# Latent attention in a decoder trunk: q left unnormalised until the exponential, the shared rotary key turned once, v copied by ScalarE, q and k signalled apart

## The chip, the core and the metric

The kernel runs on one core of a Trainium2 chip, in fp32. The metric is the device time of one execution in microseconds. A core has a matrix engine (TensorE, PE in the rows; its weight loads are listed apart as PEld), VectorE (DVE), ScalarE (ACT), GpSimd (POOL) and DMA queues, issued from SyncE (SP) and others. The engines run their own instruction streams and meet at semaphores: an instruction raises one, another engine waits until it has reached a count.

## The reference, cut to what matters

512 tokens of width 1024 pass through two layers. Layer 0 is a state-space and recurrent mixer, layer 1 is multi-head latent attention with 8 heads, and a mixture of 64 experts follows each. The change is inside the attention of layer 1:

```python
c_q = rms_norm(proj[..., :Q_LORA], cq_norm)                  # 384 wide
c_kv = rms_norm(proj[..., Q_LORA:Q_LORA + KV_LORA], ckv_norm)  # 256 wide
k_rope = proj[..., Q_LORA + KV_LORA:]                        # 64 wide, one for all heads
q = (c_q @ w_uq).reshape(bsz, seq, MLA_HEADS, QK_DIM)        # 8 heads of 128 + 64
kv = (c_kv @ w_ukv).reshape(bsz, seq, MLA_HEADS, NOPE_DIM + V_DIM)
k_nope, v = kv[..., :NOPE_DIM], kv[..., NOPE_DIM:]
k = jnp.concatenate([k_nope, jnp.broadcast_to(k_rope[:, :, None, :], ...)], axis=-1)
q = rms_norm(q, q_norm)      # one root for each token and head, over all 192
k = rms_norm(k, k_norm)
q = concat([q[..., :NOPE_DIM], apply_rope(q[..., NOPE_DIM:], cos, sin)])
k = concat([k[..., :NOPE_DIM], apply_rope(k[..., NOPE_DIM:], cos, sin)])
s = einsum(q, k) / sqrt(192); causal mask; p = softmax(s); o = p @ v
```

`apply_rope` turns the two halves of the last 64 columns: `[t1*c - t2*s, t1*s + t2*c]`.

## The kernel before

The 512 tokens are four chunks `c` of 128, one token per partition. Layer 0 and its experts run first, then `norm_tensor(2)` and `odd_tensor`, `odd_scalar`, `odd_vector`, which are the attention on TensorE, ScalarE and VectorE, then the experts of layer 1, whose weights stream from HBM.

The attention has four stages. First the input projection (line 872), with the low-rank parts normalised and transposed chunk by chunk (lines 961 to 977 and 1041 to 1047). Then, second, comes what the change is about, a list called `UNITS`. A unit is one PSUM bank of TensorE's work, and the banks are used in turn, eight of them, so that unit `u` waits until unit `u - 8` has been copied out (`copied`, line 861). For each chunk there are three units `q` (line 890, the 1536 columns of q), four units `kv` (line 894, each with k and v of two heads), and six units `t` (line 907), which transpose a finished chunk. TensorE runs q and kv of chunk `c` before `t` of chunk `c - 1`:

```python
        for c in range(TC + 1):
            if c < TC:
                UNITS += [("q", c, n) for n in range(3)] + [("kv", c, n) for n in range(4)]
            if c:
                UNITS += [("t", c - 1, n) for n in range(6)]
```

ScalarE copies the q units out (line 987), squares all of q (line 992), squares k once VectorE has copied it (line 995), squares the shared rotary key (line 997), takes the root for q and k together (line 1000), and copies the `t` units of the chunk before into the transposed q and k (lines 1005, 1007 and 1009). VectorE sums the squares of q (line 1053), copies k and v of the four kv units (lines 1059 and 1060), sums the squares of k (line 1063), and then, after the root, multiplies q and k by their roots, multiplies the rotary parts by the norm's weights and turns them, 12 tensor operations in all (lines 1072 to 1087). At the end of these, one semaphore, `s_qn`, tells that the chunk is done. TensorE waits for it ahead of `t` (line 898), and ScalarE waits for it ahead of the square of the next q (line 991), since the scratch `rt` of the rotation lies in the tile `sq` that the square writes.

The third stage is the 32 pairs of head and chunk, `n`. TensorE computes the scores (lines 923 to 925), VectorE takes the maximum and scales it (lines 1094 and 1097), ScalarE takes the exponential (line 1016) with that as its bias, VectorE divides by the sum (line 1104), TensorE transposes (line 933), ScalarE copies (line 1024), and TensorE multiplies with v (line 943). Before its first score TensorE waits until all `t` units are copied (line 909). The fourth stage is the output projection (line 441).

Three DMA issues hang on this: the weights of the output projection wait for the last kv unit (line 1815), the gains of the next norm wait for `s_qn` of the last chunk (line 1869), and the experts' first weights wait for the last score (line 1819).

Of the kernel before, what the change touches and what calls it, by code (L numbers as in the profile page):

```python
# [8 lines left out]
ALU = mybir.AluOpType  # L9
# [3 lines left out]
P = 128  # L13
# [9 lines left out]
H = 8  # L23
# [49 lines left out]
def hybrid_decoder(nc, a, out):  # L73
    ctx = ExitStack()
    with ctx:
# [657 lines left out]
        def even_gpsimd():  # L733
# [49 lines left out]
            for m in range(MT):  # L783
# [29 lines left out]
        rt = [sq[:, i * 512:(i + 1) * 512].rearrange("p (h d) -> p h d", h=2 * H) for i in range(3)]  # L813
# [5 lines left out]
                                      .rearrange("p (c d) -> p c d", c=TC) for i in range(4)]  # L819
        css, croot, crs = small(2), small(2), small(2)  # L820
# [17 lines left out]
        s_qn = sem("s_qn")  # L838
# [22 lines left out]
        def copied(u):  # L861

            kv = UNITS[u][0] == "kv"
            return (s_qv if kv else s_qa), sum((x[0] == "kv") == kv for x in UNITS[:u + 1])

        def odd_tensor():
# [11 lines left out]
            for u, (kind, c, n) in enumerate(UNITS):  # L878
# [17 lines left out]
                else:  # L896
                    if n == 0:
                        TE.wait_ge(s_qn, c + 1)
                    for j in range(4):
                        if n < 2:  # L900
                            src = qi[c % 2][:, 4 * n + j, 0:NOPE]
                        elif n < 4:
                            src = ki[c % 2][:, 4 * (n - 2) + j, :]
                        else:
                            src = rp[c % 2][:, 8 * (n - 4) + 2 * j:8 * (n - 4) + 2 * j + 2, :]\
                                .rearrange("p h d -> p (h d)")
                        last = TE.transpose(bank[:, j * P:(j + 1) * P], src, ident)
# [49 lines left out]
        def odd_scalar():  # L957
# [20 lines left out]
            for kind, c, n in UNITS:  # L978
                if kind == "kv":
                    continue  # L980
                u = unit(kind, c, n)
                bank = ps[:, u % 8, :]
                S.wait_ge(s_q, u + 1)
                if kind == "q":
# [3 lines left out]
                    if n == 2:  # L988
                        S.wait_ge(*copied(u))
                        if c:  # L990
                            S.wait_ge(s_qn, c)
                        S.activation(sq, qif[c % 2], ACT.Square).then_inc(s_hsq, 1)
                        S.wait_ge(s_hs, 3 * c + 1)
                        S.wait_ge(*copied(unit("kv", c, 3)))
# [4 lines left out]
                        S.wait_ge(s_hs, 3 * c + 3)  # L999
                        S.activation(hroot, hss, ACT.Sqrt, bias=eps, scale=1.0 / QK).then_inc(s_hr, 1)  # L1000
# [5 lines left out]
                elif n < 4:  # L1006
                    S.activation(kTn[:, 4 * (n - 2):4 * (n - 2) + 4, cc], src, ACT.Copy, scale=gnk).then_inc(s_qa, 1)
                else:
                    S.activation((qTr, kTr)[n - 4][:, :, cc], src, ACT.Copy).then_inc(s_qa, 1)
            for n in range(H * TC + 2):  # L1010
                if n < H * TC:
# [4 lines left out]
                    S.activation(pr[n % 3][:, 0:nk], ps[:, n % 3, 0:nk], ACT.Exp, scale=ATT_SCALE,  # L1016
# [9 lines left out]
        def odd_vector():  # L1026
# [13 lines left out]
            ts(ropec, ropec, -2.0, ALU.mult, 1.0, ALU.add)  # L1040
            for c in range(TC):
# [5 lines left out]
                V.nop().then_inc(s_cn, 1)  # L1047
            for c in range(TC):
# [3 lines left out]
                V.wait_ge(s_hsq, 3 * c + 1)  # L1052
                vlink(V.reduce_sum(hss[:, 0:8], sq.rearrange("p (h d) -> p h d", h=H), AX.X))
                V.nop().then_inc(s_hs, 1)
                for n in range(4):
                    u = unit("kv", c, n)
                    V.wait_ge(s_q, u + 1)
# [12 lines left out]
                rq = hrs[:, 0:8][:, :, None]  # L1070
# [4 lines left out]
                V.tensor_tensor(q_[:, :, 0:NOPE], q_[:, :, 0:NOPE], rq.to_broadcast([P, H, NOPE]), ALU.mult)  # L1075
                tt(k_, k_, rk.to_broadcast([P, H, NOPE]), ALU.mult)
                V.tensor_tensor(p_[:, 0:8, :], p_[:, 0:8, :], grq[:, None, :].to_broadcast([P, H, ROPE]), ALU.mult)
                tt(p_[:, 8:16, :], p_[:, 8:16, :], grk[:, None, :].to_broadcast([P, H, ROPE]), ALU.mult)
                cb = ropec[:, c:c + 1, :].to_broadcast([P, 2 * H, half])
                snb = ropes[:, c:c + 1, :].to_broadcast([P, 2 * H, half])  # L1080
                f1, f2 = p_[:, :, 0:half], p_[:, :, half:ROPE]
                V.tensor_tensor(rt[0], f1, snb, ALU.mult)
                tt(rt[1], f2, snb, ALU.mult)
                V.tensor_tensor(f1, f1, cb, ALU.mult)
                tt(f2, f2, cb, ALU.mult)
                V.tensor_tensor(f1, f1, rt[1], ALU.subtract)
                tt(f2, f2, rt[0], ALU.add)
                V.nop().then_inc(s_qn, 1)  # L1088
            for n in range(H * TC + 5):
                if n < H * TC:  # L1090
# [6 lines left out]
                    V.tensor_scalar(nb[:, b:b + 1], mx[:, b:b + 1], -ATT_SCALE, None, ALU.mult).then_inc(s_mx, 1)  # L1097
# [882 lines left out]
```

## Time and profile before

| | |
|---|---|
| time, 3 runs | 1644.01 us median, 1641.84 to 1645.41 |
| the profiled execution's own time | 1644.24 us |
| its span | 1642.3 us |
| TensorE busy in the span | 1351.0 us, 82% |
| units of stage two, first q to last copy | 849.94 to 943.9 us of the span |
| the 32 heads and chunks | 944.08 to 1025 us |
| output projection | from 1025.28 us |
| experts of layer 1, first expert | from about 1112 us to the end |

All starts are microseconds from the start of the span. An engine's busy share says little of the whole; what a change is worth is read from the stage in which it lies, by who waits for whom there. Idle time in square brackets stands for the time that the engine waited just before the row, with the row of another engine that released it.

### The profile page before, as it was taken

What the parts mean: (1) busy time and instruction counts of PE and PEld (TensorE: products, weight loads), DVE (VectorE), ACT (ScalarE), POOL (GpSimd) and SP (SyncE); (2) the same over time, 40 slices, a digit from 0 to 9 for tenths busy, and PEclk for the clock granted to TensorE, in tenths of its full rate; (3) what the DMA queues carried; (4) which work ended last, traced back from release to release, by engine and by line L of the source; (5) the groups of instructions that cost most, each with busy time, mean ns of one, the idle gap of its engine ahead of it and who ended that gap; (6) DMA issues with size and microseconds to landing.
All of it is one profiled execution on the core that took longest, in us unless ns stands there. A gap on an engine that the chain in (4) does not pass through costs nothing.

```text
span 1642.3 us, 19412 instructions
## 1 busy us (share of the span) xinstructions
PE 1351.0 (82%) x6152; PEld 632.2 (38%) x6152; DVE 490.5 (30%) x940; ACT 287.3 (17%) x564; POOL 316.6 (19%) x427
## 2 busy tenths in 40 slices
PE   5988995988777878788889699977988787878786
PEld 4555453333223333333544376453333232333332
DVE  6996125111111111112507654142111111111114
ACT  3235110111001010101243443111111000010100
POOL 6213001232221212121000000002332222212220
PEclk9999996999999998989889799988999999999988
DMA  6514724999999999997220301366999999999995
GB/s 210 211 46 151 298 97 160 394 387 406 402 402 399 405 395 413 401 399 290 99 109 1 116 1 63 142 256 247 393 401 401 392 402 394 409 404 403 389 382 235
DMA packets 83522, 472.36 MB, mean 288 GB/s; under 512 B 13970, under 2 KB 16194, under 8 KB 32912
## 3 DMA queue, kind: packets, MB, share of 16 engines
q1 hardware_dynamic: 69792, 445.25, 68.7%
q0 software_dynamic: 11952, 20.14, 3.8%
q10 hardware_dynamic: 1728, 6.29, 0.9%
q8 instruction: 33, 0.54, 0.1%
q14 instruction: 17, 0.14, 0.0%
HBM read 454.59 MB, written 27.39 MB: 293 GB/s over the span
## 4 chain that ended last, share of the span: by engine, by line
PE 43%; SPq 31%; DVE 13%; issue 6%; DMA 5%; ACT 2%; DVEq 0%; POOL 0%; ACTq 0%; POOLq 0%
SPq L1600 20%; PE ps L1395 14%; SPq L1605 11%; PE ps L1415 6%; DMA ring<-in_moe_w 4%; PE ps L441 3%; PE ps L1385 2%; PE ps L872 2%; PE ps L315 2%; PE ps L390 2%; PE ps L430 2%; DVE ring L541 1%; PE ps L925 1%; PE ps L943 1%; DVE extra L541 1%
## 5 line engine op out<-in xcount | busy, mean ns | idle before, releaser
L1395 PE MATMUL ps<-ring,region_b 128*64 128x512 f32 x1408 | 342.3, 642 | 79.7 <-issue 53.7
L1395 PEld LDWEIGHTS ps<-ring,region_b 128*64 128x64 f32 x1408 | 116.3, 148 | 303.1 <-issue 265.7
L1532 DVE TENSOR_TENSOR extra<-extra,ps 128x256 f32<-128x256 f32 x64 | 27.0, 421 | 609.5 <-ACT extra L1470 609.5
L1395 PE MATMUL ps<-wbuf,region_b 128*64 128x512 f32 x320 | 165.6, 678 | 48.3 <-DMA region_a<-in_moe_w 29.1
L1415 PE MATMUL ps<-ring,extra 128*64 128x512 f32 x704 | 160.8, 598 | 34.2 <-DVE extra L1538 34.2
L1395 PE MATMUL ps<-region_a,region_b 128*64 128x512 f32 x320 | 165.8, 678 | 0.0
L1339 POOL DMA_INDIRECT region_b<-hrow,icol x120 | 111.2, 927 | 148.2 <-issue 148.2
L1351 POOL DMA_INDIRECT ytok<-extra,icol x120 | 105.6, 880 | 154.1 <-issue 154.1
L1470 ACT ACTIVATE extra<-ps 128x256 f32<-128x256 f32 x64 | 24.6, 384 | 593.0 <-PE ps L1395 593.0
L1545 DVE COPY extra<-ps 128x512 f32<-128x512 f32 x64 | 44.3, 692 | 242.2 <-PE ps L1415 242.2
L1395 PEld LDWEIGHTS ps<-wbuf,region_b 128*64 128x64 f32 x320 | 48.2, 156 | 160.6 <-issue 150.1
L1415 PEld LDWEIGHTS ps<-ring,extra 128*64 128x64 f32 x704 | 49.8, 136 | 114.8 <-issue 89.7
L1349 POOL COPY icol<-blkidx 64x2 int32 x60 | 10.5, 175 | 421.4 <-DVE extra L1545 421.4
L1385 PEld LDWEIGHTS ps<-con,region_b 128*128 128x128 f32 x512 | 63.2, 195 | 64.3 <-issue 64.3
L1385 PE MATMUL ps<-con,region_b 128*128 128x128 f32 x512 | 75.7, 292 | 13.6 <-DMA region_b<-hrow,blkidx 13.6
L1415 PE MATMUL ps<-wbuf,extra 128*64 128x512 f32 x320 | 73.1, 597 | 16.7 <-DVE extra L1538 16.7
L1476 ACT ACTIVATE extra<-ps 128x512 f32<-128x512 f32 x64 | 38.2, 597 | 276.1 <-PE ps L1415 276.1
L315 PE MATMUL ps<-region_b,wbuf 128*128 128x512 f32 x128 | 55.8, 594 | 0.0
L1463 ACT ACTIVATE region_b<-ps 128x512 f32<-128x512 f32 x64 | 38.2, 597 | 81.5 <-PE ps L1385 81.5
L1839 POOL DMA_DIRECT2D gain<-in_p_norms x4 | 2.4, 600 | 252.1 <-DVEq L1088 168.7
L1527 DVE COPY region_b<-ps 128x512 f32<-128x512 f32 x64 | 44.3, 692 | 18.5 <-PE ps L1385 18.3
L1395 PEld LDWEIGHTS ps<-region_a,region_b 128*64 128x64 f32 x320 | 48.1, 156 | 0.0
(297 smaller groups left out, 1568.6 us busy)
## 6 DMA issues: line engine op xcount, KB each, us to landing
ring<-in_moe_w SPq DMA_DIRECT2D x264, 1024.0 KB, 26.3
wbuf<-in_moe_w SPq DMA_DIRECT2D x80, 1024.0 KB
region_a<-in_moe_w SPq DMA_DIRECT2D x40, 1024.0 KB
ytok<-ring SPq DMA_DIRECT2D x8, 1024.0 KB, 10.2
wbuf<-in_ev_w_in SPq DMA_DIRECT2D x3, 2048.0 KB, 17.2
wbuf<-in_ev_w_out SPq DMA_DIRECT2D x2, 2048.0 KB, 14.2
hrow<-region_a ACTq DMA_DIRECT2D x8, 512.0 KB, 10.8
region_a<-ytok SPq DMA_DIRECT2D x8, 512.0 KB, 5.3
```

The costliest lines, as they stand in the source:

```text
L315: last = TE.matmul(ps[:, bank, :], w[:, k, m * P:(m + 1) * P], hT[:, k, :], start=k == 0, stop=k == KC - 1)
L441: last = TE.matmul(ps[:, 4 + (n + 2) % 4, :], lhs(k, n // 2), wout[n % 2][:, k, :], start=k == 0, stop=k == KC - 1)
L1339: G.indirect_dma_start(xin[j][CAP * g:CAP * g + n, :], None, hrow[l], bass.IndirectOffsetOnAxis(ap=icol[0:n, 2 * j + g:2 * j + g + 1], axi ...
L1351: G.indirect_dma_start(ytok[l], bass.IndirectOffsetOnAxis(ap=icol[0:n, 4 + 2 * j + g:5 + 2 * j + g], axis=0), yo[j][CAP * g:CAP * g + n, : ...
L1385: last = TE.transpose(ps[:, k // 4, (k % 4) * PAIR:(k % 4 + 1) * PAIR], xin_block(j, k), ident)
L1395: last = TE.matmul(ps[CAP * g:CAP * (g + 1), 2 + j, :], xtr[j][:, k, CAP * g:CAP * (g + 1)], up_weights(2 * slot + g, k), start=k == 0, st ...
L1415: last = TE.matmul(ps[CAP * g:CAP * (g + 1), 6 + nh, :], hidT[j][:, f, CAP * g:CAP * (g + 1)], w2[2 * slot + g][:, f * D + nh * 512:f * D ...
L1463: S.activation(xtr[j][:, 4:8, :].rearrange("p k s -> p (k s)"), ps[:, 1, :], ACT.Copy)\
L1527: V.tensor_copy(xtr[j][:, 0:4, :].rearrange("p k s -> p (k s)"), ps[:, 0, :])\
L1545: V.tensor_copy(yo[j][:, 0:512], ps[:, 6, :]).then_inc(ml["s_ye"][l], 1)
L1600: nc.sync.dma_start(w13[b][:, n, :], src).then_inc(s, 16)
L1605: nc.sync.dma_start(w2[b], src).then_inc(s, 16)
```

## The change

It has five parts.

- q is no longer multiplied by its root. The scores come out of TensorE too large by it, and since a query is a partition there, the root goes in as the exponential's scale, one number per partition, `scl[:, n:n + 1]` in place of a constant, and as the factor of the maximum (`nscl`). Two operations of 128x8 for each chunk fill these tables.
- The norm's weights on the rotary part of q go into four tables (`qcc`, `qss`, `qcs`, `qsc`), made once. The rotation of q is then 6 operations of 128x256 that read the q copied out and wait for no root. Its scratch `rt` lies in `cbuf`, no longer in `sq`.
- The shared rotary key is weighted and turned once for all four chunks and before any root (`krot`, 8 operations of 128x128). For each chunk one operation of 128x512 spreads it over the heads with their roots.
- v is copied out by ScalarE, after VectorE has copied k of the same bank. All units then count on one semaphore, `s_qa`.
- `s_qn` is raised when q is turned, ahead of the sums for k, and a new one, `s_kn`, when k is scaled. The `t` units are reordered to q, q, rotary q, k, k, rotary k, and TensorE waits for `s_qn` ahead of the first and for `s_kn` ahead of the fourth. ScalarE's square of the next q waits for `s_hs`, the counter of VectorE's sums, and no longer for `s_qn`. The root (`keys_root`) moves behind the first two `t` copies of the chunk before, except for chunk 0.

The diff, cut to its core:

```diff
-        rt = [sq[:, i * 512:(i + 1) * 512].rearrange("p (h d) -> p h d", h=2 * H) for i in range(3)]
+        rt = [cbuf[:, i * 256:(i + 1) * 256].rearrange("p (h d) -> p h d", h=H) for i in range(2)]
+        scl, nscl = extra[:, 4032:4064], extra[:, 4064:4096]
...
         def copied(u):
 
-            kv = UNITS[u][0] == "kv"
-            return (s_qv if kv else s_qa), sum((x[0] == "kv") == kv for x in UNITS[:u + 1])
+            return s_qa, u + 1
...
-                    if n == 0:
-                        TE.wait_ge(s_qn, c + 1)
+                    if n % 3 == 0:
+                        TE.wait_ge((s_qn, s_kn)[n // 3], c + 1)
...
+            def keys_root(c):
+                S.wait_ge(s_hs, 3 * c + 3)
+                S.activation(hroot, hss, ACT.Sqrt, bias=eps, scale=1.0 / QK).then_inc(s_hr, 1)
...
                         if c:
-                            S.wait_ge(s_qn, c)
+                            S.wait_ge(s_hs, 3 * c)
                         S.activation(sq, qif[c % 2], ACT.Square).then_inc(s_hsq, 1)
+                    continue
+                if kind == "kv":
+                    kvs += 1
+                    S.wait_ge(s_qv, kvs)
+                    S.activation(vbuf[:, c, 2 * n * VD:(2 * n + 2) * VD].rearrange("p (h d) -> p h d", h=2),
+                                 bank.rearrange("p (h d) -> p h d", h=2)[:, :, NOPE:NOPE + VD], ACT.Copy)\
+                        .then_inc(s_qa, 1)
+                    if n == 3:
                         S.wait_ge(s_hs, 3 * c + 1)
-                        S.wait_ge(*copied(unit("kv", c, 3)))
                         S.activation(sq[:, 0:H * NOPE], kif[c % 2], ACT.Square).then_inc(s_hsq, 1)
...
-                        S.wait_ge(s_hs, 3 * c + 3)
-                        S.activation(hroot, hss, ACT.Sqrt, bias=eps, scale=1.0 / QK).then_inc(s_hr, 1)
+                        if c == 0:
+                            keys_root(c)
...
+                if n == 1 and c + 1 < TC:
+                    keys_root(c + 1)
...
-                    S.activation(pr[n % 3][:, 0:nk], ps[:, n % 3, 0:nk], ACT.Exp, scale=ATT_SCALE,
+                    S.activation(pr[n % 3][:, 0:nk], ps[:, n % 3, 0:nk], ACT.Exp, scale=scl[:, n:n + 1],
...
+            V.wait_ge(s_ct, TC)
+            V.tensor_tensor(k1, kro[:, :, 0:half], gains(grk, 0), ALU.mult)
+            tt(k2, kro[:, :, half:ROPE], gains(grk, 1), ALU.mult)
...
-                    V.tensor_copy(k_[:, 2 * n:2 * n + 2, :], src[:, :, 0:NOPE])
-                    V.tensor_copy(vbuf[:, c, 2 * n * VD:(2 * n + 2) * VD].rearrange("p (h d) -> p h d", h=2),
-                                  src[:, :, NOPE:NOPE + VD]).then_inc(s_qv, 1)
+                    V.tensor_copy(k_[:, 2 * n:2 * n + 2, :], src[:, :, 0:NOPE]).then_inc(s_qv, 1)
+                V.tensor_tensor(rt[0], t2, turn(qss), ALU.mult)
+                V.tensor_tensor(rt[1], t1, turn(qcs), ALU.mult)
+                V.tensor_tensor(f1, t1, turn(qcc), ALU.mult)
+                tt(f2, t2, turn(qsc), ALU.mult)
+                V.tensor_tensor(f1, f1, rt[0], ALU.subtract)
+                V.tensor_tensor(f2, f2, rt[1], ALU.add).then_inc(s_qn, 1)
...
-                V.tensor_tensor(p_[:, 0:8, :], q_[:, :, NOPE:QK], rq.to_broadcast([P, H, ROPE]), ALU.mult)
-                V.tensor_tensor(p_[:, 8:16, :], kro[:, c:c + 1, :].to_broadcast([P, H, ROPE]),
+                V.tensor_tensor(p_[:, 8:16, :], krot[:, c:c + 1, :].to_broadcast([P, H, ROPE]),
                                 rk.to_broadcast([P, H, ROPE]), ALU.mult)
...
+                V.tensor_tensor(k_, k_, rk.to_broadcast([P, H, NOPE]), ALU.mult).then_inc(s_kn, 1)
+                V.tensor_scalar(scl[:, 8 * c:8 * c + 8], hrs[:, 0:8], ATT_SCALE, None, ALU.mult)
+                ts(nscl[:, 8 * c:8 * c + 8], hrs[:, 0:8], -ATT_SCALE, ALU.mult)
...
-                    V.tensor_scalar(nb[:, b:b + 1], mx[:, b:b + 1], -ATT_SCALE, None, ALU.mult).then_inc(s_mx, 1)
+                    V.tensor_scalar(nb[:, b:b + 1], mx[:, b:b + 1], nscl[:, n:n + 1], None, ALU.mult).then_inc(s_mx, 1)
```

VectorE's row in stage two, one chunk of the kernel before, from the sum of q's squares (`smalls<-extra`) on; `ring` holds q and k of the chunk, `region_a` is v, `ps` is PSUM:

```order
L1053 TENSOR_REDUCE smalls<-extra 128x8 [waits s_v,s_hsq]
...
L1063 TENSOR_REDUCE smalls<-extra 128x8 [waits s_hsq]
L545 TENSOR_SCALAR smalls<-smalls 128x8 [waits s_v,s_hsq]
L1069 RECIPROCAL smalls<-smalls 128x16 [waits s_v,s_hr]
L1072 TENSOR_TENSOR ring<-ring,smalls 128x512 [waits s_v]
L1073 TENSOR_TENSOR ring<-extra,smalls 128x512
L1075 TENSOR_TENSOR ring<-ring,smalls 128x8x128
L541 TENSOR_TENSOR ring<-ring,smalls 128x1024
L1077 TENSOR_TENSOR ring<-ring,smalls 128x512 [waits s_v]
```

The same chunk of the changed kernel on VectorE:

```order
L1092 COPY ring<-ps 128x256 [waits s_q] x3
L1097 TENSOR_TENSOR extra<-ring,gain 128x256
L1098 TENSOR_TENSOR extra<-ring,gain 128x256
L1099 TENSOR_TENSOR ring<-ring,gain 128x8x32
L541 TENSOR_TENSOR ring<-ring,gain 128x8x32
L1101 TENSOR_TENSOR ring<-ring,extra 128x8x32 [waits s_v]
L1102 TENSOR_TENSOR ring<-ring,extra 128x8x32
L1104 TENSOR_REDUCE smalls<-extra 128x8 [waits s_hsq]
L545 TENSOR_SCALAR smalls<-smalls 128x8 [waits s_v,s_hsq]
L1110 RECIPROCAL smalls<-smalls 128x16 [waits s_v,s_hr]
L1112 TENSOR_TENSOR ring<-gain,smalls 128x512 [waits s_v]
L1114 TENSOR_TENSOR ring<-ring,smalls 128x1024
```

The rotation of q now stands between the copies of k and the sum of k's squares, and behind the root only two large operations remain (then the two of 128x8).

ScalarE's row in the last chunk of the kernel before, from the copies of q to the table load for the exponential:

```order
L987 ACTIVATE ring<-ps 128x512 [waits s_q] x3
L992 ACTIVATE extra<-ring 128x1536 [waits s_qn,s_qa]
L995 ACTIVATE extra<-ring 128x1024 [waits s_qv,s_hs]
L997 ACTIVATE extra,smalls<-extra 128x64 [waits s_hs]
L1000 ACTIVATE smalls<-smalls 128x16 [waits s_hs]
L1005 ACTIVATE ring<-ps,smalls 128x4x128 [waits s_q] x2
L1007 ACTIVATE ring<-ps,smalls 128x4x128 [waits s_q] x2
L1009 ACTIVATE ring<-ps 128x4x128 [waits s_q] x2
```

The same stretch of the changed kernel:

```order
L991 ACTIVATE ring<-ps 128x512 [waits s_q] x3
L996 ACTIVATE extra<-ring 128x1536 [waits s_hs,s_qa]
L1001 ACTIVATE region_a<-ps 128x256 [waits s_qv,s_q] x4
L1006 ACTIVATE extra<-ring 128x1024 [waits s_hs]
L1008 ACTIVATE extra,smalls<-extra 128x64 [waits s_hs]
L1016 ACTIVATE ring<-ps,smalls 128x4x128 [waits s_q] x2
L982 ACTIVATE smalls<-smalls 128x16 [waits s_hs]
L1020 ACTIVATE ring<-ps 128x4x128 [waits s_q]
L1018 ACTIVATE ring<-ps,smalls 128x4x128 [waits s_q] x2
L1020 ACTIVATE ring<-ps 128x4x128 [waits s_q]
```

Four copies of v came in, the root (line 982) stands behind two of the transposed copies, and the square of q waits for another counter.

## Rows read from the trace of the kernel before

**Rows 1.** The page's groups: busy, mean ns, idle before.

```profile
L1470 ACT ACTIVATE extra<-ps 128x256 f32<-128x256 f32 x64 | 24.6, 384 | 593.0 <-PE ps L1395 593.0
```

**Rows 2.** Windows: stretch, length, busy PE, PEld, DVE, ACT, POOL, granted clock, DMA.

```profile
886.20:905.30 19.10, 17.92 (x59) 9.03 (x58) 14.95 (x25) 7.95 (x14) 0.00 (x0) 1.00 0.00 1
...
924.40:938.00 13.60, 0.08 (x2) 0.08 (x2) 11.09 (x17) 5.00 (x10) 0.00 (x0) 0.56 0.64 239
...
944.00:965.00 21.00, 20.92 (x122) 16.15 (x122) 12.23 (x52) 9.90 (x38) 0.00 (x0) 1.00 0.00 1
```

**Rows 3.** Timeline of TensorE and its weight loads: start, length, idle before.

```profile
881.45 1.91 PE L907 MATMUL ps<-con,ring 128*128 128x128 f32 x16
884.91 1.32 PE L907 MATMUL ps<-con,ring 128*128 128x128 f32 x8 [1.55 <-DVE region_a L1060]
886.24 7.99 PE L890 MATMUL ps<-wbuf,ring 128*128 128x512 f32 x18
...
900.93 1.91 PE L907 MATMUL ps<-con,ring 128*128 128x128 f32 x16
...
920.03 1.91 PE L907 MATMUL ps<-con,ring 128*128 128x128 f32 x16
...
937.95 5.36 PE L907 MATMUL ps<-con,ring 128*128 128x128 f32 x24 [13.52 <-DVEq L1088]
944.08 0.46 PE L923 MATMUL ps<-ring 128*128 128x128 f32 x2 [0.78 <-ACT ring L1009]
...
881.45 1.67 PEld L907 LDWEIGHTS ps<-con,ring 128*128 128x128 f32 x15 [0.29 <-issue]
```

**Rows 4.** Timeline of VectorE and ScalarE in the last chunk.

```profile
924.63 0.41 DVE L1060 COPY region_a<-ps 128x256 f32<-128x256 f32 x1
926.22 1.22 DVE L1063 TENSOR_REDUCE smalls<-extra 128x8 f32<-128x1024 f32 x1 [1.18 <-ACT extra L995]
928.87 0.69 DVE L1072 TENSOR_TENSOR ring<-ring,smalls 128x512 f32<-128x512 f32 x1
...
937.06 0.69 DVE L541 TENSOR_TENSOR ring<-ring,extra 128x512 f32<-128x512 f32 x1
...
927.53 0.26 ACT L997 ACTIVATE extra<-extra 128x64 f32<-128x64 f32 x1 [1.34 <-DVEq L1064]
...
928.24 0.31 ACT L1000 ACTIVATE smalls<-smalls 128x16 f32<-128x16 f32 x1 [0.36 <-DVEq L1067]
```

**Rows 5.** Groups, shapes apart, 840 to 945 us: busy, mean ns, idle before.

```profile
L1005 ACT ACTIVATE ring<-ps,smalls 128x512 f32<-128x512 f32 x8 | 5.1, 677 | 7.4 <-PE ps L907 7.4
L541 DVE TENSOR_TENSOR ring<-ring,smalls 128x1024 f32<-128x1024 f32 x4 | 4.9, 1220 | 0.0
L1009 ACT ACTIVATE ring<-ps 128x512 f32<-128x512 f32 x8 | 4.5, 613 | 0.4 <-PE ps L907 0.4
...
L1082 DVE TENSOR_TENSOR extra<-ring,gain 128x512 f32<-128x512 f32 x4 | 2.8, 692 | 0.1
```

**Rows 6.** Groups, shapes apart, 944 to 1025 us.

```profile
L1024 ACT ACTIVATE extra<-ps 128x128 f32<-128x128 f32 x8 | 2.1, 268 | 0.0
...
L1016 ACT ACTIVATE ring<-ps,smalls 128x128 f32<-128x128 f32 x5 | 1.8, 368 | 3.0 <-DVE smalls L1097 3.0
```

**Rows 7.** Waits of TensorE from 944 to 1025 us: total, times, longest.

```profile
PE ps L923 <- ACT ring L1009: 0.8, 1, 0.8
```

**Rows 8.** Windows of one microsecond: the same columns as in the second group.

```profile
854.00:855.00 1.00, 1.00 (x3) 0.42 (x2) 0.00 (x0) 0.00 (x0) 0.00 (x0) 0.76 0.00 0
...
926.00:927.00 1.00, 0.00 (x0) 0.00 (x0) 0.78 (x1) 0.19 (x1) 0.00 (x0) 0.58 1.05 395
...
943.00:944.00 1.00, 0.31 (x2) 0.00 (x0) 0.00 (x0) 0.73 (x3) 0.00 (x0) 0.89 0.00 0
```

**Rows 9.** Timeline of VectorE: two rows that start after long idle times.

```profile
828.74 0.17 DVE L1043 RECIPROCAL smalls<-smalls 128x2 f32<-128x2 f32 x1 [23.19 <-ACT smalls L970]
...
862.34 1.75 DVE L1053 TENSOR_REDUCE smalls<-extra 128x8 f32<-128x1536 f32 x1 [15.46 <-ACT extra L992]
```

More of the change, by code:

```diff
@@ L819, in hybrid_decoder @@
                                       .rearrange("p (c d) -> p c d", c=TC) for i in range(4)]
+        qcc, qss, qcs, qsc = [gain[:, 512 + i * 128:640 + i * 128].rearrange("p (c d) -> p c d", c=TC) for i in range(4)]
+        krot = gain[:, 0:256].rearrange("p (c d) -> p c d", c=TC)
         css, croot, crs = small(2), small(2), small(2)
@@ L837, in hybrid_decoder @@
         s_hr = sem("s_hr")
-        s_qn = sem("s_qn")
+        s_qn, s_kn = sem("s_qn"), sem("s_kn")
         s_sc = sem("s_sc")
@@ L977, in odd_scalar @@
                 S.nop().then_inc(s_cte, 1)
[L978 to L981, printed above, removed]
+            def keys_root(c):
+                S.wait_ge(s_hs, 3 * c + 3)
+                S.activation(hroot, hss, ACT.Sqrt, bias=eps, scale=1.0 / QK).then_inc(s_hr, 1)
+            kvs = 0
+            for u, (kind, c, n) in enumerate(UNITS):
                 bank = ps[:, u % 8, :]
@@ L1005, in odd_scalar @@
                     S.activation(qTn[:, 4 * n:4 * n + 4, cc], src, ACT.Copy, scale=gnq).then_inc(s_qa, 1)
-                elif n < 4:
-                    S.activation(kTn[:, 4 * (n - 2):4 * (n - 2) + 4, cc], src, ACT.Copy, scale=gnk).then_inc(s_qa, 1)
-                else:
-                    S.activation((qTr, kTr)[n - 4][:, :, cc], src, ACT.Copy).then_inc(s_qa, 1)
+                elif n in (3, 4):
+                    S.activation(kTn[:, 4 * (n - 3):4 * (n - 3) + 4, cc], src, ACT.Copy, scale=gnk).then_inc(s_qa, 1)
+                else:
+                    S.activation((qTr, kTr)[n // 3][:, :, cc], src, ACT.Copy).then_inc(s_qa, 1)
+                if n == 1 and c + 1 < TC:
+                    keys_root(c + 1)
             for n in range(H * TC + 2):
@@ L1040, in odd_vector, with gains @@
             ts(ropec, ropec, -2.0, ALU.mult, 1.0, ALU.add)
+            def gains(g, i):
+                return g[:, None, i * half:(i + 1) * half].to_broadcast([P, TC, half])
+            V.tensor_tensor(qcc, ropec, gains(grq, 0), ALU.mult)
+            V.tensor_tensor(qss, ropes, gains(grq, 1), ALU.mult)
+            V.tensor_tensor(qcs, ropes, gains(grq, 0), ALU.mult)
+            tt(qsc, ropec, gains(grq, 1), ALU.mult)
             for c in range(TC):
@@ L1047, in odd_vector @@
                 V.nop().then_inc(s_cn, 1)
+            k1, k2 = [cbuf[:, i * 128:(i + 1) * 128].rearrange("p (c d) -> p c d", c=TC) for i in range(2)]
+            k3, k4 = [cbuf[:, 256 + i * 128:384 + i * 128].rearrange("p (c d) -> p c d", c=TC) for i in range(2)]
+            V.wait_ge(s_ct, TC)
+            V.tensor_tensor(k1, kro[:, :, 0:half], gains(grk, 0), ALU.mult)
+            tt(k2, kro[:, :, half:ROPE], gains(grk, 1), ALU.mult)
+            V.tensor_tensor(k3, k2, ropes, ALU.mult)
+            V.tensor_tensor(k4, k1, ropes, ALU.mult)
+            V.tensor_tensor(krot[:, :, 0:half], k1, ropec, ALU.mult)
+            tt(krot[:, :, half:ROPE], k2, ropec, ALU.mult)
+            V.tensor_tensor(krot[:, :, 0:half], krot[:, :, 0:half], k3, ALU.subtract)
+            tt(krot[:, :, half:ROPE], krot[:, :, half:ROPE], k4, ALU.add)
             for c in range(TC):
@@ L1868, in _ @@
                     router(1)
-                    g.wait_ge(s_qn, TC)
+                    g.wait_ge(s_kn, TC)
                     row_gain(3)
```

32 lines of the change are left out of this document (11 added, 21 removed).

## The prediction

> **What bounds the kernel now.** The whole span says little, since the change touches one stage, so I read the stage by windows first, then by timelines. In stage two TensorE is busy 17.92 us of a chunk's period of 19.10 us, VectorE 14.95 and ScalarE 7.95 [rows 2]. So nothing is full, and the period is set by a circle of waits: the square of q waits for `s_qn`, which ends VectorE's 12 large operations, which wait for the root, which waits for k's squares, which wait for the copies of k and v, which stand behind the sum of q's squares. TensorE meets this circle at one place in each chunk, 1.55 us of idle time before the fifth `t` unit in the first of them, released by VectorE's late copy of v [rows 3]. Note how thin that is: even a perfect circle lets TensorE gain little there, because the rest of its period is work.
>
> The large idle time is behind the last kv unit. TensorE has nothing but the last six `t` units left and waits 13.52 us for VectorE to end its chain [rows 3]. The reader should see in the timeline of VectorE that from 928.87 to 937.75 us it does nothing but the 12 operations of 128x512 and 128x1024 [rows 4]. The `t` units then run at a granted clock of 0.5 (1.2 GHz), since the clock had fallen at 926 to 927 us after TensorE stopped [rows 8], and the first score starts at 944.08 us [rows 3]. After this TensorE is busy 20.92 of 21.00 us [rows 2], and in the whole of stage three it waits once, 0.8 us, at its first score [rows 7]: stage three is TensorE's.
>
> **What is removed, and where it counts.** I take TensorE's row from 881.45 us on, the end of the second chunk's kv units, since before that the change moves nothing that TensorE waits for: the first chunk's k and v copies and its square come in the same order, and two chunks' units go out before any `t`.
>
> *The middle.* One stretch of q and kv units takes 900.93 - 886.24 = 14.69 us [rows 3], all work. Six `t` units without a stall take 24 transposes at 1.67/15 = 0.111 us, that is 2.67 us [rows 3]. Before, the way from 881.45 us to the end of the last kv unit at 920.03 was 38.58 us. If TensorE never waits it is 2 x (2.67 + 14.69) = 34.72 us. Gain **3.9 us**. For this the other engines have to keep up. VectorE's chain for a chunk becomes 1.75 for the first sum, 4 copies at 0.41, 6 rotations, 1.22, 0.69 and 1.22 [rows 4, 5, 9], under 10 us in all. The rotations are of 128x256 and the trace has no such row from SBUF; half of the 0.69 of 128x512 is the floor, the 0.41 of a 128x256 copy from PSUM the ceiling [rows 4, 5], and I take 0.36, so six are 2.2 us (2.1 to 2.5). ScalarE gains four copies of v, at most the 0.384 us that it takes for a 128x256 tile from PSUM [rows 1], 1.5 us on 7.95. Both stay far under 17.4 us. The copy of v that frees the bank of the fifth `t` unit now comes 0.4 us behind the copy of k, some 4 us ahead of TensorE.
>
> *The tail.* I follow the last chunk from the end of its last kv unit (time 0). Copy of k, 0.2 to notice it and 0.4: 0.6. Six rotations: 2.8, and here `s_qn` rises, just as TensorE ends the chunk before's `t` units at 2.67. Sum of k's squares, 1.22 [rows 4]: 4.0. ScalarE's square of the rotary key starts 0.1 later and takes 0.26 and a read of 0.19; then come two transposed copies of 0.68, which overlap by about 0.1 [rows 4, 5]: 5.6. Root 0.31 [rows 4]: 5.9. Reciprocal with its waits 0.3, the rotary key 0.69 and k 1.22, overlapping by 0.1 [rows 5]: 8.1, and `s_kn` rises. ScalarE has seven transposed copies to do from 5.9 on, at 0.61 or 0.68 less the overlap, done at 9.7. TensorE's last three `t` units start at 8.15 and, if the clock is low as it was before, take 5.36/6 = 0.89 each [rows 3], done at 10.8; the last copy follows in 0.2 and 0.6. So the first score starts at **11.6** behind the last kv unit. With a warm clock it is ScalarE's queue that ends last, at nearly the same time. Before, it was 944.08 - 920.03 = 24.05 us [rows 3]. Gain **12.4 us**.
>
> **What is added.** The 4 operations for q's tables lie in 23.19 us that VectorE idles, the 8 for the rotary key in the 15.46 us ahead of the first sum [rows 9]. At 0.3 to 0.7 us each they cost nothing; without the cover they would be 4 to 5 us. The scales of 128x8, two for each chunk, follow `s_kn`; nothing on the tail waits for them but the first maximum's scaling 3 us later. The loads of the output projection's weights and the next norm's gains start earlier by what is gained, and have stage three to land in.
>
> In stage three the exponential reads its scale as a column, as it does its bias already. The nearest pair of rows is the exponential of 128x128 with one such column, 368 ns, against a copy without, 268 [rows 6], and scaled against unscaled transposed copies, 677 against 613 [rows 5]. So each of the 32 may grow by up to 0.1 us, and the sum over all would be 3.2 us. I cost it at nothing but 0.1 at the last head, because TensorE waits for no exponential there [rows 7]. The Trainium skill says the same against the change more sharply ("ScalarE: Activation LUTs", What ACT_TABLE_LOAD costs): each pointer operand of an ACTIVATE adds about 93 ns. By that page, if all were exposed, the 32 would cost 3.0 us; the trace's 100 ns for a first column agrees with it, and the idle times decide.
>
> *The clock.* In the changed tail TensorE works in pieces (two `t` units at 2.8, one at about 5.3, three at 8.15). Before, the clock was seen falling 1.5 to 2.5 us after TensorE stopped at 924.4, and it rose at about 943.1, 5 us into the last `t` units [rows 3, 8]. It rose at about 854.5, too [rows 8], after the stage's first matrix work at 849.94 (the table above). I expect it low at 8.15 and still low when the scores begin. Before, all of the rise was paid in the `t` units; now 1.5 to 5 us of stage three run at 1.2 GHz, at half speed, which costs 0.7 to 2.4 us, or nothing if the clock never falls. I take **1.2 us**.
>
> Sum: -3.9 - 12.4 + 0.1 + 1.2 = **-15.0 us**. Everything later (output projection, the experts' weights, which start at the last score) hangs on the end of stage three and moves with it. Against the profiled execution's own 1644.24 us this gives 1629.2. The median of the runs shown is 0.2 below it, so I say **1629.0 us**.
>
> **The rivals.**
>
> - *The middle doesn't tighten.* ScalarE's row is a strict order, and the root, the transposed copies and the copies of v are now in one line; if one of them is late, a bank is late for TensorE, and the period stays at 19.1. Then only the tail is gained, less 1.2: 12.4 - 1.3 = 11.1, 1632.9 us. Against it speak 4 us of slack at the fifth `t` unit, and ScalarE's copies of the first `t` units, done about 2.5 us before TensorE needs their banks. Chance 0.13.
> - *The columns are on the path.* Heads with 128 keys are short, and there the exponential may be waited for. All 32 exposed give 3.1 us more than I counted, 1632.1. (The page "ScalarE: Activation LUTs" of the Trainium skill, cited above, would make it 2.9.) Against it: no wait in the rows. Chance 0.07.
> - *The clock costs nothing,* or VectorE's rotations are at their floor and handovers are quicker: 1627.5 us. Chance 0.15.
> - *Slower.* The clock, having fallen in a broken tail, stays at 1.2 GHz through the heads. Half speed over t us costs t/2, so it decides against the change when it lasts over some 32 us of stage three, and over all 81 us it would cost 40 and give 1669. Against it: in the trace before it came back within 5.5 us of steady work both times, and stage three is steady work. Chance 0.02.
> - *The waits are not what the trace shows,* and the tail is hidden behind something else, such as the 4 MB of the output projection's weights. Their issue waits for the last kv unit at 920.03 us [rows 3], and they are wanted after 1025, so 90 us of slack speak against it. No change, 1644. Chance 0.03.
>
> **How the numbers follow.** The forecast has 0.60. From 1626.3 us (clock and rotations both at the good end, 12.4 + 3.9 - 0.1 + 0.5 = 16.7 saved, and 1 us of scatter between runs) to 1633.9 us (the middle doesn't tighten, and as much scatter) it holds over 8 in 10. Changes under 0.2%, 3.3 us, can't be told from none. Faster by more: all but the last two rivals, 0.95. Same 0.03, slower 0.02.
>
> **What would show it.** In the changed profile TensorE should have no idle time from 850 us to the end of the third chunk's `t` units, a period near 17.4 us, kv of the last chunk ending at about 916.2, and the first score at about 927.8. VectorE's `s_qn` should stand 2.8 us behind the last kv unit and ScalarE's last transposed copy should end the tail. The exponentials should be up to 0.1 us longer each while TensorE waits for none, and one-microsecond windows should show the clock low from about 924 to about 930 us. Wrong would be: a wait of TensorE on a bank in the middle, a longer stage three than 81.2 us plus the clock's share, or rotations over 0.5 us each.

## The result

The changed kernel takes 1630.63 us (median of 4 runs, 1627.96 to 1632.39) against 1644.28 us of the kernel before: a ratio of 0.992, interval 0.9907 to 0.9933, so 13.6 us faster. Six more runs of it, later, gave 1632.63 us and 0.9929, 0.9917 to 0.9941. The forecast was 1629.0 in 1626.3 to 1633.9. Both medians lie in that range; against the runs of the kernel before that were taken with them, the six are 11.0 us faster, so the gain is known to some 2 us.

The profiled execution took 1629.92 us, with a span of 1628.1 us. The timeline of TensorE in the changed kernel, from the second chunk's last kv unit to the first scores, answers to [rows 3] (line 909 is the `t` units, 892 q, 896 kv, 925 the scores):

```profile
882.36 2.78 PE L909 MATMUL ps<-con,ring 128*128 128x128 f32 x24
884.98 7.89 PE L892 MATMUL ps<-wbuf,ring 128*128 128x512 f32 x18
892.70 7.03 PE L896 MATMUL ps<-region_b,ring 128*128 128x512 f32 x16
899.57 2.78 PE L909 MATMUL ps<-con,ring 128*128 128x128 f32 x24
...
916.78 3.97 PE L909 MATMUL ps<-con,ring 128*128 128x128 f32 x32
921.74 0.66 PE L909 MATMUL ps<-con,ring 128*128 128x128 f32 x4 [0.99 <-ACT ring L1016]
924.75 2.79 PE L909 MATMUL ps<-con,ring 128*128 128x128 f32 x12 [2.35 <-DVE ring L1114]
928.32 0.77 PE L925 MATMUL ps<-ring 128*128 128x128 f32 x2 [0.78 <-ACT ring L1020]
```

There is no idle time up to 920, and behind it three short waits (0.99, 2.35 and 0.78 us), where the kernel before waited 1.17, 13.52 and 0.78 us. Windows over two chunks, stage three and what lies between it and the experts (the same columns as in [rows 2]) show the rest:

```profile
882.36:899.57 17.21, 17.21 (x59) 9.03 (x58) 9.05 (x18) 9.31 (x18) 0.00 (x0) 1.00 0.00 1
899.57:916.78 17.21, 17.21 (x59) 9.03 (x58) 9.05 (x18) 9.31 (x18) 0.00 (x0) 1.00 0.00 0
928.32:1013.63 85.31, 84.24 (x432) 58.52 (x433) 42.12 (x136) 34.44 (x97) 0.00 (x0) 0.95 0.10 37
1013.63:1105.24 91.61, 73.28 (x258) 41.68 (x259) 33.04 (x96) 10.72 (x20) 3.81 (x4) 0.88 0.52 209
```

and the same two later stretches of the kernel before:

```profile
944.08:1025.28 81.20, 80.28 (x432) 55.36 (x433) 40.27 (x136) 31.66 (x97) 0.00 (x0) 1.00 0.07 27
1025.28:1116.75 91.47, 73.29 (x259) 41.68 (x259) 33.05 (x96) 10.72 (x20) 3.81 (x4) 0.87 0.52 210
```

TensorE fills its period of 17.21 us completely; VectorE's busy time in a period fell from 14.95 to 9.05 us. Stage three got 4.1 us longer at a mean clock of 0.95. The 14.2 us between the spans are made up like this:

| stretch | before | after | difference |
|---|---|---|---|
| up to the second chunk's last kv unit | 881.45 | 882.36 | +0.9 |
| from there to the last kv unit ("middle") | 38.58 | 34.42 | -4.2 |
| from there to the first score ("tail") | 24.05 | 11.54 | -12.5 |
| stage three, to the output projection | 81.20 | 85.31 | +4.1 |
| to the first expert of layer 1 | 91.47 | 91.61 | +0.1 |
| from there to the end | 525.55 | 522.86 | -2.7 |

The first and the last row are taken as scatter. Over all fourteen profiles of this study the first lies between 880.8 and 887.8 us and the last between 522.4 and 525.6, and neither follows the edits. The kernel before alone has runs from 1639.31 to 1646.80 us. So a whole time says little of an edit worth 1 or 2 us, and the experiments are read by three rows, the middle, the tail and stage three, which repeat to within about 0.1 us wherever the clock is the same. These three rows give 12.6 us of gain in this profile, where the forecast had 15.0.

### The profile page after: what moved, and what is told of

It is laid out like the page before. It is cut to its first block, busy times and chain, and to the rows that moved or that the text cites. A ratio compares the mean times of both kernels' runs of the same rounds, so it can differ in the third digit from the quotient of the medians.

```text
span 1628.1 us, 19431 instructions
## 1 busy us (share of the span) xinstructions
PE 1352.6 (83%) x6152; PEld 635.0 (39%) x6152; DVE 471.4 (29%) x928; ACT 294.7 (18%) x580; POOL 316.6 (19%) x427
## 4 chain that ended last, share of the span: by engine, by line
PE 46%; SPq 31%; DVE 10%; issue 6%; DMA 5%; ACT 2%; DVEq 0%; POOL 0%; POOLq 0%; ACTq 0%
SPq L1628 20%; PE ps L1423 13%; SPq L1633 11%; PE ps L1443 6%; DMA ring<-in_moe_w 4%; PE ps L441 3%; PE ps L892 2%; PE ps L874 2%; PE ps L315 2%; PE ps L896 2%; PE ps L390 2%; PE ps L430 2%; PE ps L1413 2%; PE ps L927 2%; PE ps L925 1%
## 5 line engine op out<-in xcount | busy, mean ns | idle before, releaser
L1423 PE MATMUL ps<-wbuf,region_b 128*64 128x512 f32 x320 | 161.8, 664 | 45.4 <-DMA region_a<-in_moe_w 29.8
L1423 PE MATMUL ps<-region_a,region_b 128*64 128x512 f32 x320 | 162.0, 665 | 0.0
L1377 POOL COPY icol<-blkidx 64x2 int32 x60 | 10.5, 175 | 418.5 <-DVE extra L1573 418.5
L1357 POOL DMA_INDIRECT region_b<-hrow,blkidx x8 | 8.6, 1080 | 198.5 <-DVE blkidx L1322 196.7
```

Of the source, the lines that this page charges most:

```text
L1423: last = TE.matmul(ps[CAP * g:CAP * (g + 1), 2 + j, :], xtr[j][:, k, CAP * g:CAP * (g + 1)], up_weights(2 * slot + g, k), start=k == 0, st ...
```

## The experiments

Theory one: the chain of work on VectorE and ScalarE set middle and tail, and what stage three lost is the clock. Each experiment undoes or adds one or two things, and most expectations name a rival. Four of the kernels have one run each, the profiled one: one signal (1631.10 us), the old place of the wait (1631.28), v on VectorE (1635.87) and the shared key for each chunk (1633.05). Of these only the rows are read.

**Fillers for the clock.** Three matmuls whose results nobody reads go into TensorE's waits in the tail of the changed kernel:

```diff
+                    if c == TC - 1 and n == 3:
+                        for j in range(2):
+                            TE.matmul(bank, ident, tcount, start=True, stop=True)
                     if n % 3 == 0:
                         TE.wait_ge((s_qn, s_kn)[n // 3], c + 1)
...
                 TE.wait_ge(*copied(u))
+                if u == len(UNITS) - 8:
+                    TE.matmul(ps[:, u % 8, 0:384], ident, tcount[:, 0:384], start=True, stop=True)
```

> The changed kernel, with three matmuls added on TensorE whose results nobody reads, in the last chunk's idle times: two of 128x512 between the rotary q transposes and the wait for s_kn, one of 128x384 ahead of the first score. Theory one, stage three of the changed kernel is 4.1 us longer than before (85.3 us against 81.2, first score to output projection) because it begins with the clock at 1.2 GHz until 937 us: then the clock stays high, stage three takes 81.2 to 81.8 us again, and the time falls by 3 to 4 us against the changed kernel, to about 1627. Theory two, the exponential's and the maximum's scale read as a column are on the path: stage three stays at 85 us and the time at 1630 to 1631.

Its tail on TensorE, with the fillers in lines 901 and 917:

```profile
927.75 1.98 PE L901 MATMUL ps<-con 128*128 128x512 f32 x4
930.10 1.53 PE L912 MATMUL ps<-con,ring 128*128 128x128 f32 x12 [0.36 <-DVE ring L1119]
931.46 0.81 PE L917 MATMUL ps<-con 128*128 128x384 f32 x2
933.46 0.46 PE L930 MATMUL ps<-ring 128*128 128x128 f32 x2 [1.18 <-ACT ring L1025]
```

Middle 34.43, tail 11.25, stage three 81.58 us. The clock stays at 1.00 through the tail, and stage three is back to within 0.4 us of the 81.20 before. The whole time was 1629.53 us (ratio 0.9911, 0.9897 to 0.9924): the medians don't tell it from the changed kernel, the stage does.

**Constants for the columns.** `scale=ATT_SCALE` in the exponential, `-ATT_SCALE` for the maximum.

> The changed kernel with constants in place of the columns, in the exponential's scale and in the scaling of the maximum, so q's root is left out of the result. Theory one (the clock): nothing changes, stage three 85.3 us, within 0.3. Theory two (the columns): the exponential of 128x128 falls from 457 to 368 ns and the maximum's scaling from 214 to 154, and stage three falls by 32 x 0.15 = 4.8 us at most, by 2 at least.

Stage three 85.13 us, 1630.02 us in all (ratio 0.9913, 0.9898 to 0.9928). The exponentials had grown as foreseen, yet taking the columns away gives 0.2 us. Groups of the changed kernel in stage three, which answer to [rows 6], and one of the maximum's scaling:

```profile
L1125 DVE TENSOR_SCALAR smalls<-smalls,extra 128x1 f32<-128x1 f32 x32 | 6.9, 214 | 1.1
...
L1029 ACT ACTIVATE ring<-ps,smalls,extra 128x128 f32<-128x128 f32 x5 | 2.3, 457 | 5.3 <-DVE smalls L1125 5.3
```

457 against 368 ns is 89 ns for the second column. By the Trainium skill ("ScalarE: Activation LUTs", What ACT_TABLE_LOAD costs) it is about 93 ns; the row agrees. With the clock high, kernels with the columns take 81.58 to 81.70 us and the one without 81.20, so they cost 0.4 to 0.5 us in all. They show at the ends of the stage alone: in the kernel with fillers the eighth head starts 0.19 us later behind the first than in the kernel before, the last one 0.22, and 0.16 more come behind the last score.

**One signal for TensorE.** `TE.wait_ge(s_kn, c + 1)` ahead of the first and the fourth `t` unit.

> The changed kernel, in which TensorE waits for s_kn ahead of the first t unit as well, as if q and k had one signal. Theory one, the middle is TensorE's row without gaps and both signals are long up there: the end of the last kv unit doesn't move (34.4 us behind the second chunk's), and only the tail grows, since six t units instead of three stand behind s_kn: three more at 0.89 us at the low clock, 2.7 us, less what ScalarE had still to copy, so 2 to 2.7 us more from last kv unit to first score (13.6 to 14.3 instead of 11.5). Rival, the separate signal is what freed the middle: the period goes back toward 19.1 us and the last kv unit comes 2 to 4 us later.

Middle 34.43, tail 14.10 as expected, and then a surprise: stage three 81.59 us. The timeline of its tail shows why:

```profile
926.37 5.35 PE L909 MATMUL ps<-con,ring 128*128 128x128 f32 x24 [5.19 <-DVE ring L1114]
932.50 0.46 PE L925 MATMUL ps<-ring 128*128 128x128 f32 x2 [0.78 <-ACT ring L1020]
```

Its six units run in one piece at the low clock, and the clock rises just behind their end (the window from 932 to 933 us has a mean of 0.86), as it did near their end in the kernel before [rows 8], so that the scores start high. The window:

```profile
932.00:933.00 1.00, 0.50 (x4) 0.52 (x4) 0.00 (x0) 0.98 (x2) 0.00 (x0) 0.86 0.38 143
```

The separate signal won 2.6 us in the tail and lost 3.7 behind it; in these two profiles q's own signal to TensorE cost 1.2 us. One profile of each kernel doesn't say how often that is so.

**The old place of the wait.** ScalarE's square of q waits for `s_kn` instead of `s_hs`.

> The changed kernel, in which ScalarE's square of the next q waits for s_kn, the end of VectorE's chain, as it waited for s_qn before. Theory one, the circle was broken by its length and not by this wait: s_kn rises about 907 us and the third copy of the next q is done at about 910.7, so nothing waits, all stage times stay within 0.1 us. Rival, the looser wait is what freed the middle: each period grows by 1 us or more.

Middle 34.42, tail 11.54, stage three 85.38 us: nothing moved. The new wait bought nothing.

**The root alone.** On the kernel before:

```diff
-                V.tensor_tensor(p_[:, 0:8, :], q_[:, :, NOPE:QK], rq.to_broadcast([P, H, ROPE]), ALU.mult)
...
-                V.tensor_tensor(q_[:, :, 0:NOPE], q_[:, :, 0:NOPE], rq.to_broadcast([P, H, NOPE]), ALU.mult)
...
-                V.tensor_tensor(p_[:, 0:8, :], p_[:, 0:8, :], grq[:, None, :].to_broadcast([P, H, ROPE]), ALU.mult)
+                V.tensor_tensor(p_[:, 0:8, :], q_[:, :, NOPE:QK], grq[:, None, :].to_broadcast([P, H, ROPE]), ALU.mult)
```

with `scl` and `nscl` filled and read as in the change.

> The kernel before with one part of the change: q's root goes into the exponential's scale and the maximum's factor, so VectorE's two multiplications of q by its root (128x512 and 128x1024) are gone; the rotations, the copies of v, the one signal and the waits stay. Theory one, VectorE's chain behind the root sets period and tail: it is 1.7 us shorter, so TensorE's idle time in the middle (1.2 to 1.55 us a chunk) goes, the last kv unit ends about 2.5 us earlier against the second chunk's, and the tail from last kv unit to first score is 24.05 - 1.7 = 22.3 us or a little more. 4 us in all, 1640. Rival, it is the copies of v on VectorE that make TensorE wait, and the middle keeps 38.6 us.

1637.65 us, ratio 0.9957 (0.994 to 0.9973). Middle 35.22, tail 20.60, stage three 81.70 us. The middle gained 3.4 us, 0.9 more than expected, and 0.8 us of waiting is left in it; the tail gained 3.45 us, twice the 1.7 by which the chain is shorter. VectorE's rows tell why. Its last copy of v, line 1061 here:

```profile
918.50 2.78 PE L908 MATMUL ps<-con,ring 128*128 128x128 f32 x24
...
921.38 0.42 DVE L1061 COPY region_a<-ps 128x256 f32<-128x256 f32 x1
```

It ends 3.3 us behind the last kv unit, where the kernel before ended it 5.0 us behind [rows 3, 4]. From its end to the last six `t` units there are 11.2 us (they start at 932.97), where there were 12.9 [rows 3, 4]. So the 1.7 us count twice in the tail: the chain is shorter, and it starts earlier behind TensorE. It had started late because the circle, 19.1 us a round, was longer than TensorE's own 17.2, so that VectorE lagged behind; with the root alone a round takes 17.4 us.

**v on VectorE again.** ScalarE's copy becomes an empty instruction that only raises `s_qa`.

> The changed kernel with v copied by VectorE again, behind k, bank by bank. Theory one, VectorE has room in the middle: no wait of TensorE there, the way from second to last chunk's kv end stays at 34.4 us, and the tail grows only by what the last copy of v puts ahead of the rotation, 0.3 to 0.4 us. Rival, the move to ScalarE carries the middle: it goes back toward 38.6 us.

Middle 34.43, tail 11.87, both as expected: the move of v is worth 0.3 us. But stage three took 89.66 us, since the clock returned at 948 us.

**The shared key for each chunk.** `kro` times root and weights and six operations of rotation, behind the root.

> The changed kernel with the shared rotary key weighted and turned for each chunk again, behind the root: one more operation of 128x512 and six of 128x256 on VectorE ahead of s_kn, 0.6 + 6 x 0.34 and the waits between, 2.9 us. Theory one, VectorE has room in the middle: from the second to the last kv unit's end 34.4 us as in the changed kernel, and the tail grows by 2.5 to 3 us, to 14.0 to 14.5. Rival: the middle feels it too, and TensorE waits for s_kn or a bank in each chunk.

Middle 34.43, tail 14.76, stage three 85.37 us. The tail grew by 3.2 us, a little more than expected, and the middle doesn't feel it.

**Two early steps.** VectorE's six rotations of q stand ahead of the sum of q's squares, behind a wait for q's third copy, and ScalarE's square of the rotary key loses its wait for the sum of k's squares:

```diff
-                        S.wait_ge(s_hs, 3 * c + 2)
                         S.activation(sq[:, 1024:1024 + ROPE], kro[:, c, :], ACT.Square, accum_out=krss)\
```

> The changed kernel with two steps moved to where their engine idles: VectorE turns q right after q is copied, ahead of the sum of q's squares, and ScalarE squares the shared rotary key right after k's square, without waiting for the sum of k's squares. By my reading of the tail both are on its path: the sum of k's squares starts 0.6 us earlier, and the root waits no longer for a round trip to ScalarE, about 1.1 us. ScalarE's queue of transposed copies then ends the tail. Last kv unit to first score falls from 11.5 to 9.5 to 10.2 us. If ScalarE's queue alone already ended it, nothing changes. The clock is as in the changed kernel, low at the first score, and stage three stays at about 85 us.

Tail 9.64 us, as expected, stage three 86.13 us. The whole times didn't follow: ten runs from 1629.40 to 1645.21 us, median 1635.15, ratio 0.9959 (0.9935 to 0.9984). A tail 1.9 us shorter gave no faster kernel and a wider spread. It was run again:

> The kernel with the two early steps again, unedited. Theory one, the clock comes back at different times in stage three, 9 us or some 30 us after the first score: the spread recurs, with runs from 1628 to 1645 us, and if the profiled run is one of the long ones its stage three shows a granted clock of 0.5 for 20 us or more. Theory two, the ten runs of before were disturbed by something else on that chip: the runs lie within 1626 to 1631.

Eight runs, 1627.87 to 1642.14, median 1632.19, ratio 0.9942 (0.992 to 0.9963): the spread recurs, but the median is that of the changed kernel on the same chip (1632.63, next experiment), so only the spread is shown, not that it is slower. The profiled one was of 1632.83 us, with tail and stage three as in the first profile, so no long run was caught in a trace.

**The changed kernel again.**

> The changed kernel again, unedited, in more runs. Theory one: the clock's return after the broken tail is not fixed; in one profile it came at 937 us, 9 us into stage three, and in the profile with v on VectorE at 948. Then the times spread toward one side, with some runs several us above the fastest, as they did for the kernel with the two early steps (1629 to 1645 us over ten runs), while the kernel before stays within its 5 us. Theory two: that spread belongs to the two early steps alone, and this one stays within 1627 to 1633.

1632.63 us, 1629.91 to 1637.16. The longest of these runs was the profiled one. Windows of it, with nothing edited:

```profile
924.00:928.00 4.00, 2.65 (x12) 2.42 (x12) 1.36 (x4) 4.00 (x8) 0.54 (x1) 0.51 1.05 388
928.00:932.00 4.00, 3.22 (x12) 2.44 (x11) 0.51 (x2) 2.37 (x5) 0.00 (x0) 0.50 0.90 341
932.00:936.00 4.00, 4.00 (x14) 3.10 (x15) 1.72 (x8) 1.34 (x6) 0.00 (x0) 0.50 0.01 5
936.00:940.00 4.00, 4.00 (x16) 3.33 (x17) 1.72 (x8) 1.11 (x5) 0.00 (x0) 0.50 0.00 0
940.00:944.00 4.00, 4.00 (x16) 3.10 (x15) 1.01 (x5) 1.04 (x6) 0.00 (x0) 0.50 0.00 0
944.00:948.00 4.00, 4.00 (x16) 3.37 (x15) 1.57 (x8) 1.43 (x6) 0.00 (x0) 0.50 0.00 0
948.00:952.00 4.00, 4.00 (x21) 2.87 (x21) 2.65 (x9) 1.44 (x6) 0.00 (x0) 1.00 0.01 2
```

and of the first profile of the same kernel:

```profile
932.00:936.00 4.00, 4.00 (x15) 3.06 (x15) 1.72 (x8) 1.26 (x5) 0.00 (x0) 0.50 0.00 0
936.00:940.00 4.00, 4.00 (x24) 3.50 (x25) 2.29 (x11) 1.48 (x7) 0.00 (x0) 0.83 0.00 0
940.00:944.00 4.00, 4.00 (x25) 3.01 (x24) 2.10 (x10) 2.09 (x9) 0.00 (x0) 1.00 0.00 0
```

Middle and tail are the same to the hundredth, 34.42 and 11.54. The clock came back 19 us behind the first score instead of 9, and stage three took 89.71 us instead of 85.31. TensorE ran without a gap meanwhile, in both. What differs ahead of it is small: by windows of one microsecond the clock fell about 1.3 us into the wait of 2.35 us in the first profile and about 1.1 us into it in this one. Why the one return is 10 us later stays open.

**The best version.** The early steps, the two fillers of 128x512, and the last two transposed copies given to VectorE:

```diff
-            for u in range(len(UNITS) - 8, len(UNITS)):
+            TE.wait_ge(s_qn, TC + 2)
+            for u in range(len(UNITS) - 8, len(UNITS) - 2):
+                TE.wait_ge(*copied(u))
...
+                if n == 4:
+                    V.tensor_scalar(kTn[:, 4:8, cc], src, gnk, None, ALU.mult).then_inc(s_qn, 1)
+                else:
+                    V.tensor_copy(kTr[:, :, cc], src).then_inc(s_qn, 1)
```

First without this split, with all three fillers:

> The two steps moved early and the three filler matmuls together. If both readings are right they add up: tail 9.5 to 10.2 us, stage three 81.2 to 81.8 us, in all 5 to 5.5 us less than the changed kernel, about 1625.

1627.40 us, 1623.73 to 1628.00, ratio 0.9892 (0.9876 to 0.9909); tail 9.63, stage three 81.58. Then with it:

> The two early steps, the two filler matmuls of 128x512 ahead of the wait for s_kn, and the last two transposed copies of the last chunk given to VectorE, which idles there. ScalarE's queue ended the tail in the profile with early steps and fillers (9.63 us from last kv unit to first score). With two copies less it should end 0.5 to 1.1 us earlier: 8.5 to 9.1 us. Stage three 81.2 to 81.8 us with the clock high. The time falls to 1624 to 1627, in a narrow spread; under theory one of the clock, this and the other kernel with fillers are the ones without long runs.

1624.44 us, 1623.27 to 1624.63, ratio 0.988 (0.9865 to 0.9894), against 0.9929 (0.9917 to 0.9941) for the changed kernel on the same chip: 8.2 us faster than it. Tail 8.89, stage three 81.62. Its timeline of TensorE, and then a window at the start of stage three:

```profile
918.08 4.09 PE L912 MATMUL ps<-con,ring 128*128 128x128 f32 x36
...
922.01 1.88 PE L901 MATMUL ps<-con 128*128 128x512 f32 x4
...
924.36 1.53 PE L912 MATMUL ps<-con,ring 128*128 128x128 f32 x12 [0.47 <-DVE ring L1120]
...
926.97 0.49 PE L929 MATMUL ps<-ring 128*128 128x128 f32 x2 [1.08 <-DVE ring L1131]
```

The window:

```profile
928.00:932.00 4.00, 4.00 (x24) 3.06 (x24) 2.79 (x13) 1.83 (x8) 0.00 (x0) 1.00 1.02 387
```

Line 901 is the fillers (the third, ahead of the first score, is left out here, and stage three keeps its time without it); behind them the last three `t` units take 1.53 us where they took 2.79, and the clock is at 1.00 where it was at 0.50.

The stages side by side, all read from the starts of the same four rows of TensorE:

| kernel | middle | tail | stage three |
|---|---|---|---|
| before | 38.58 | 24.05 | 81.20 |
| before, root alone | 35.22 | 20.60 | 81.70 |
| changed | 34.42 | 11.54 | 85.31 |
| changed, again | 34.42 | 11.54 | 89.71 |
| constants | 34.43 | 11.54 | 85.13 |
| square after k | 34.42 | 11.54 | 85.38 |
| one signal | 34.43 | 14.10 | 81.59 |
| v on VectorE | 34.43 | 11.87 | 89.66 |
| key for each chunk | 34.43 | 14.76 | 85.37 |
| fillers | 34.43 | 11.25 | 81.58 |
| early steps | 34.42 | 9.64 | 86.13 |
| early steps, fillers | 34.43 | 9.63 | 81.58 |
| early, fillers, split | 34.43 | 8.89 | 81.62 |

## Why the prediction held, point by point

*The middle* (-3.9 forecast, -4.2 measured) was right in mechanism and size; the stretch of q and kv units took 14.59 instead of 14.69 us, since the q units behind the stall took 7.99 us [rows 3] and the others 7.89. The root alone brings 3.4 of the 4.2. v's move and the looser wait of the square, each undone alone, move nothing in it.

*The tail* (-12.4 forecast, -12.5 measured) was right step by step, counted from 916.78 us:

```profile
917.33 0.41 DVE L1097 TENSOR_TENSOR extra<-ring,gain 128x256 f32<-128x256 f32 x1
...
919.12 0.42 DVE L1102 TENSOR_TENSOR ring<-ring,extra 128x256 f32<-128x256 f32 x1
...
922.16 0.30 ACT L982 ACTIVATE smalls<-smalls 128x16 f32<-128x16 f32 x1
```

Rotations took 0.42 us each, 0.34 apart; `s_qn` rose 2.8 us behind the last kv unit, and the root started at 5.4 and ended at 5.7, where 5.9 was forecast. Of the gain, the root alone gives 3.45 us, taking the shared key out of the chunk 3.2, TensorE's separate signal 2.6 and v 0.3. If these add up, the other 3.0 us were not run alone; by elimination they belong to what is left, q's rotation with its weights, now shorter and ahead of the root, which is argued and not shown. The root was taken out of the kernel before and the others were undone in the changed one, so the sum itself is a reckoning. What the prediction did not see is the lag of the circle, a part of the 24.05 us.

*The covers* held. The tables, the early turn of the key, the output projection's weights: no wait on any of them in the trace.

*The columns* (+0.1 forecast) cost 0.2 at the low clock and 0.4 to 0.5 at the high one: right in mechanism, a little too small.

*The clock* is the term that was mis-sized. "I take 1.2 us" stood in the sum, with 2.4 as the bound from returns seen within 5.5 us; measured are 3.7 (85.31 less the 81.58 with fillers) in one profile and 8.1 in another of the same kernel. The forecast's own sign, a clock low to about 930 us, failed: it was low to 937. The bound failed because the time in which the clock had come back behind other work was carried over to this tail. In both places that it came from, TensorE had worked in one piece behind its idle time, and on other work than the scores (long matmuls of q, and 24 transposes). Which of the two matters, the breaks or the kind of work, no run separates: the fillers keep the clock from falling, and with one signal it is back before the scores. The forecast's time came out well partly because the last stretch was 2.7 us shorter in this pair of profiles, by chance. And the rival given 0.02, a clock that stays low far into the heads, is real as a mechanism: it lasted 19 us of the 32 from which it would decide. That it makes the runs of 1640 to 1645 us with early steps is argued from their spread (17 us over 18 runs, against 7.5 us for the kernel before, over more runs) and from the narrow one with early steps and fillers (1623.27 to 1628.00 us over 8 runs), not seen in a trace. The mean granted clock of each run points the same way, 0.920 to 0.923 in the seven runs over 1638 us and 0.922 to 0.929 in the other eleven. But the groups' means differ by 0.004, where a low clock that explained all of the 10.5 us between them would make about 0.006 (an estimate: 21 us more at half the clock in 1640), so a part may be something else.

## What to carry to other kernels

When a chain on the vector engines circles through several chunks, compare its period with the matrix engine's own: as long as the chain's is longer, each microsecond saved counts in every chunk, beyond that only in the tail, and a lag that has built up is paid there too. A wait that is cut into pieces can leave the matrix engine in short bursts, and the next stage then begins at 1.2 GHz for a time that differs from run to run; so compare the granted clock in the first microseconds behind a tail, over more than one profile, and try to fill idle time of a few us with matmuls nobody reads (here they gave stage three 3.7 us back), or to keep the work in one piece (stage three as short, but the tail 2.6 us longer). Read stages, not medians, where the parts that are not touched scatter by more than the edit.

## What the runs showed of the hardware

The clock's return is not a fixed time behind the work. With six transposing units in one piece it rose about 5.3, 5.5 and 5.9 us after they began (by windows of one microsecond), in the kernel before, with the root alone and with one signal, each time before the first score. Where the units came in pieces and nothing filled the waits between them, it rose during the scores, with no gap in TensorE's row from the first score on: 9.0 to 9.2 us behind the first score in four profiles (changed, constants, square after k, key for each chunk), 11.1 us in the two with early steps, and 19.0 and 19.1 us in two (v on VectorE, changed again). Two of these eight are of one kernel, unedited, with 9 and 19 us, and TensorE's rows from the second chunk's last kv unit to the first score are alike in them to 0.01 us.
